# Spreading a normalisation's two parameter rows with TensorE instead of broadcasting them by DMA

## The reference

```python
def layer_norm(x, g, b):
    xf = x.astype(jnp.float32)
    mu = jnp.mean(xf, axis=-1, keepdims=True)
    var = jnp.mean(jnp.square(xf - mu), axis=-1, keepdims=True)
    y = (xf - mu) * lax.rsqrt(var + LN_EPS)
    return (y * g.astype(jnp.float32) + b.astype(jnp.float32)).astype(x.dtype)
...
    h = layer_norm(x, ln_in_g, ln_in_b)
    for l in range(DEPTH):
        h = hybrid_layer(h, ...)          # begins with x @ w_in, w_in: 1024 x IN_WIDTH
```

## Time and profile before

| | us |
|---|---|
| three runs | 2106.35, 2108.43, 2108.76 (median 2108.43) |
| the profiled execution | 2107.81 |
| its span | 2106.1 |
| PE busy in the span | 2041.2 (97%) |
| DVE, ACT, POOL busy | 1495.8, 1187.7, 715.4 |
| mean granted clock of TensorE | 0.997 of full |

### The profile page before, as it was taken

The page is one execution under the profiler, slowest core; times in us unless marked ns, Lnnn a source line. Parts: engine busy times, 40 slices in busy tenths (PEclk is TensorE's granted clock), DMA queues, the critical chain, the costliest instruction groups (busy, mean ns, idle before and its releaser), DMA issues.

```text
span 2106.1 us, 36550 instructions
## 1 busy us (share of the span) xinstructions
PE 2041.2 (97%) x11636; PEld 1744.8 (83%) x11636; DVE 1495.8 (71%) x2958; ACT 1187.7 (56%) x2023; POOL 715.4 (34%) x646
## 2 busy tenths in 40 slices
PE   8999999999999999999999999999999999999997
PEld 6987888888887888788788888888888878888886
DVE  6666768888888655655676567788888886555556
ACT  4456457766657644545444554567755685554443
POOL 1100005877874311111120000088787561111111
PEclk9999999999999999999999999999999999999999
DMA  5654546777773467667565734477777615766664
GB/s 187 205 181 132 178 151 180 188 182 189 189 183 103 134 215 226 209 223 227 178 200 169 228 114 153 166 181 189 187 183 189 186 59 182 218 221 219 226 221 144
DMA packets 179781, 384.12 MB, mean 182 GB/s; under 512 B 52528, under 2 KB 85328, under 8 KB 179696
## 3 DMA queue, kind: packets, MB, share of 16 engines
q1 hardware_dynamic: 139632, 372.26, 54.4%
q0 software_dynamic: 40064, 10.81, 6.3%
HBM read 365.04 MB, written 17.96 MB: 182 GB/s over the span
## 4 chain that ended last, share of the span: by engine, by line
PE 86%; DVE 5%; DMA 4%; ACT 2%; issue 1%; POOL 0%; SPq 0%; POOLq 0%; DVEq 0%; ACTq 0%
PE wide L1689 35%; PE acc L1675 9%; PE wide L1675 9%; PE acc L1676 5%; PE wide L1676 5%; PE acc L1663 3%; PE acc L1664 3%; PE acc L1665 3%; PE acc L2171 3%; DMA raw<-in_front 2%; PE acc L1678 1%; PE wide L1678 1%; ACT hi L680 1%; DMA gt<-table 1%; PE tr L1867 1%
## 5 line engine op out<-in xcount | busy, mean ns | idle before, releaser
L680 ACT ACTIVATE hi<-raw 128x1024 fp32r<-128x1024 f32 (+1 forms) x644 | 676.1, 1050 | 641.8 <-DMA raw<-in_peer_v 335.1
L1029 DVE TENSOR_TENSOR lo<-raw,hi 128x1024 fp32r<-128x1024 f32 x520 | 635.4, 1222 | 388.0 <-ACT hi L680 386.6
L623 POOL DMA_INDIRECT table<-picks,spots x256 | 478.7, 1870 | 263.5 <-DVE spots L1499 138.6
L1675 PE MATMUL acc<-xT,hi 128*128 128x512 f32 x896 | 321.8, 398 | 0.0
L1689 PE MATMUL wide<-hi,w_lo 128*128 128x512 f32 x1016 | 314.1, 390 | 7.3 <-DVE w_lo L1603 7.0
L1675 PE MATMUL wide<-xT,hi 128*128 128x512 f32 x868 | 311.8, 398 | 4.3 <-DVE lo L1029 4.2
L1689 PE MATMUL wide<-lo,w_hi 128*128 128x512 f32 x1016 | 313.1, 389 | 0.0
L656 POOL TENSOR_TENSOR big<-big,gt 128x128 f32 x248 | 119.5, 482 | 569.8 <-DMA gt<-table 558.0
L1689 PE MATMUL wide<-hi,w_hi 128*128 128x512 f32 x1016 | 313.1, 389 | 0.0
L1676 PE MATMUL acc<-xT,lo 128*128 128x256 f32 x1024 | 266.5, 281 | 0.0
L1676 PE MATMUL wide<-xT,lo 128*128 128x256 f32 x992 | 258.2, 281 | 0.0
(11 more groups left out here) (330 smaller groups left out, 3032.9 us busy)
## 6 DMA issues: line engine op xcount, KB each, us to landing
raw<-in_peer_u SPq DMA_DIRECT2D x256, 512.0 KB, 3.5
raw<-in_peer_v SPq DMA_DIRECT2D x254, 512.0 KB, 4.4
raw<-in_front SPq DMA_DIRECT2D x114, 512.0 KB, 3.7
table<-blank SPq DMA_DIRECT2D x16, 1024.0 KB, 7.5
gt<-table SPq DMA_DIRECT2D x254, 64.0 KB, 4.1
ln_par<-in_ln POOLq DMA_DIRECT2D x10, 512.0 KB, 5.9
raw<-in_front SPq DMA_DIRECT2D x12, 384.0 KB, 3.1
w<-in_cmp_w POOLq DMA_DIRECT2D x16, 256.0 KB, 4.2
```

The lines of the kernel that those rows point to most:

```text
L623: pool.indirect_dma_start(table[l], bass.IndirectOffsetOnAxis(spots[:, u, k:k + 1], 0), picks[:, 2, 0, u * TOPK + k:u * TOPK + k + 1], Non ...
L680: nc.scalar.activation(hi[:, s, :width], raw[:, s, :width], ACT.Identity).then_inc(hi_done, 1)
L1029: nc.vector.tensor_tensor(lo[:, s], raw[:, s], hi[:, s].bitcast(F32), ALU.subtract).then_inc(lo_done, 1)
L1675: mm(bank, hi[:, s, c], xT[:, :, k], start=k == 0, stop=False)
```

## The change

The two DMAs now bring one row each to partition 0 of `ln_par` (2 x 4 KB instead of 2 x 512 KB written). POOL first writes a row of 128 ones into `first_i[0:1, 0]` and raises `pool_step`. PE, before its twenty matmuls, waits for the row of ones and for both DMAs, and multiplies the ones (as the stationary operand, 1 x 128) by the rows (as the moving operand, 1 x 512), four matmuls in plain float32: the factors go to both banks of `acc`, the shifts to both banks of `wide[:, 1]`. It then raises `ln_spread`. DVE reads factors and shifts for this first norm from PSUM. Since `acc[:, 1]` is now taken, the twenty matmuls write into `wide[:, 0]`, and ahead of the twelve later ones (into `acc[:, 1]`) PE waits in layer 0 until DVE has read the factors for the second time. The later norms load `ln_par` as before.

```diff
@@ gpsimd
-            pst = Steps(pool, pool_step, 0, 12)
-
-            def ln_load(i):
-                for r in range(2):
-                    pool.dma_start(ln_par[:, r], t["ln"][i, r].partition_broadcast(P)).then_inc(ln_loaded, 16)
-
-            ln_load(0)
+            pst = Steps(pool, pool_step, 0, 13)
+
+            for r in range(2):
+                pool.dma_start(ln_par[0:1, r], t["ln"][0, r].unsqueeze(0)).then_inc(ln_loaded, 16)
+            pst.link(nc.gpsimd.memset(first_i[0:1, 0], 1.0))
             pst.link(nc.gpsimd.memset(ident[:], 0.0))
@@ vector: normalise(tt, nth, loads, chain, meanwhile=None)
-                dve.wait_ge(ln_loaded, loads)
+                if loads is None:
+                    dve.wait_ge(ln_spread, 1)
+                    factor, shift = acc[:].rearrange("p b n -> p (b n)"), wide[:, 1]
+                else:
+                    dve.wait_ge(ln_loaded, loads)
+                    factor, shift = ln_par[:, 0], ln_par[:, 1]
                 chain.link(nc.vector.scalar_tensor_tensor(out=xs[:, tt], in0=xs[:, tt], scalar=mv[:, tt, 0:1],
-                                                          in1=ln_par[:, 0], op0=ALU.subtract, op1=ALU.mult))
+                                                          in1=factor, op0=ALU.subtract, op1=ALU.mult))
...
-                                                   in1=ln_par[:, 1, half], op0=ALU.mult, op1=ALU.add).then_inc(x_ready, 1)
+                                                   in1=shift[:, half], op0=ALU.mult, op1=ALU.add).then_inc(x_ready, 1)
@@ tensor
+            pe_.wait_ge(pool_step, 1)
+            pe_.wait_ge(ln_loaded, 32)
+            for r, dst in enumerate((acc[:].rearrange("p b n -> p (b n)"), wide[:, 1])):
+                for h in range(2):
+                    half = slice(512 * h, 512 * h + 512)
+                    ins = mm(dst[:, half], first_i[0:1, 0], ln_par[0:1, r, half], start=True, stop=True)
+            ins.then_inc(ln_spread, 1)
             pe_.wait_ge(consts_ready, 1)
             pe_.wait_ge(masks_ready, 2)
...
-            keep_clock(acc[:, 1], 20)
+            keep_clock(wide[:, 0, :512], 20)
...
                 acc_free(l, A_LAT + 1)
+                if l == 0:
+                    pe_.wait_ge(ln_step, TT * 4)
                 keep_clock(acc[:, 1], 12)
```

More of the change, by code:

```diff
@@ L442, in build @@
         stored = sem("stored")
+        ln_spread = sem("ln_spread")
         low_copied = sem("low_copied")
@@ L1094, in _ @@
                 statistics(tt, chain)
-                normalise(tt, tt, 32, chain, first_low_parts if tt == 1 else None)
+                normalise(tt, tt, None, chain, first_low_parts if tt == 1 else None)
             chain.end()
```

## The result

Nine runs of each kernel: 2114.1 us median (2112.0 to 2118.1) for the changed kernel, 2108.1 (2105.8 to 2111.1) for the one before. The ratio is 1.0033 (95% interval 1.0024 to 1.0042): 6.0 us slower by the medians, 7.0 by the ratio, where I had forecast 2110.4 with a range up to 2113.2. The sign of the shift in my sum was right, its size was not (+6.0 against +2.3), and rival 3 (2113.8, chance 0.10) is what came, together with a later landing of the rows.

A forecast was written before the change was run, and what follows sets the result against it. PE, busy 2041.2 of 2106.1 us, was taken to bound the kernel, its twenty unread matmuls the start. Adding +2.3 us on PE's chain to 2107.8 and 2108.43 (2110.1, 2110.7) gave 2110.4 us, range 2107.4 to 2113.2.

The forecast's parts named there:

- my sum: Over the whole kernel: +2.3 us on PE's chain from the start, the other parts of the change adding nothing.
- rival 3: At the start: four one-row matmuls don't raise PE's clock, the twenty start cold; +5.6 us, time 2113.8; chance 0.10.
- The bound of the start: First tile: PE's twenty unread matmuls run until 14.49; VectorE's 2.88 us wait has 1.7 to 2.4 us of slack.
- Four float32 matmuls: Ahead of PE's twenty: 1.72 us each at 1.2 GHz, some 0.95 at 2.4 GHz; the four cost 6.3 us.
- the clock should rise 5.6 us later, at 11.5: At PE's start: clock rises 5.6 us after its first matmul at 5.9, so the twenty take 4.6 us.
- the forecast of the transposes (16.8): First tile: PE gets to its transposes at 16.8 instead of 14.49, +2.3 us.
- The landing at 5.9: At the start: the two rows on POOL's queue land at 5.9 us, with 3.9 and 6.2 as ends.
- my upper end of 6.2: At the start: latest time in us taken for the landing of the two rows.
- Hidden work: Early in the kernel: new wait, memset (about 0.3 us), PSUM inputs and less early traffic add nothing to PE's chain.
- Carried to the end: From the start to the kernel's end: +2.3 us stays, since every later link hangs on PE.

The follow-up runs named there:

- the last kernel: Changed kernel with rows loaded first by SyncE, cast by VectorE, float32r spreading, 14 unread matmuls, none before layer 0's second transposes: 2106.5 us, ratio 0.9997 against kernel before.

## Why the prediction was wrong, point by point

- *The bound of the start is PE's unread matmuls, not VectorE's wait.* Right: VectorE's wait grew from 2.9 to 7.2 us and was still covered, and with the traffic taken away and PE left alone the time stayed (1.0003). The slack was small, though: with 14 unread matmuls the chain runs through `ln_par`'s transfers.
- *Four float32 matmuls, each four times a float32r one, as two records.* Right: 0.85 us a record, 1.71 a matmul, 7.1 with the first gap. The float32r form of the same work took a quarter.
- *"If they begin at 5.9, PE's first work lies 1.3 us earlier than before (7.20), and the clock should rise 5.6 us later, at 11.5."* **This is the step that failed.** I let any matmul count towards the rise and held the twenty at 4.6 us. In every trace with work of one row ahead of the twenty the rise came behind that work: here the four ran slowly to the end (7.1 instead of 6.3 us), and the twenty began at the low clock (6.8 instead of 4.6). That is 3.0 of the 4.2 us between the forecast of the transposes (16.8) and their start (21.05). With 128 rows in the same place both took 9.7 us together, where I had said 10.9 and the changed kernel took 13.9. It is rival 3 by its own mechanism. I gave it 0.10 though I wrote that the trace held no row for or against it: without a row, nothing spoke for the other side either.
- *The landing at 5.9.* Off by 1.2 us (PE starts at 7.13), the rest of the 4.2. The bytes came when I said, from 5 us on, but the last of the queue's 64 packets started only after 6.2; I took the end of the wait too near to the first bytes, and my upper end of 6.2 was too low. Why these few bytes took so long is not shown.
- *Hidden work*: the new wait ahead of the twelve, the memset, PSUM as an input, the earlier traffic. Right, none shows.
- *Carried to the end.* Right for this loss: 6.6 at the transposes, 6.4 at the 48 matmuls, 6.0 between the medians (5.1 to 8.9 by the interval). It isn't a rule for gains: 5.2 us gained at the 48 matmuls in the last kernel were 1.1 at the end (at most 2.5 by the interval). My reason, that every later link hangs on PE, leaves out that a weight tile can then be the later one.

## What to carry to other kernels

Before moving work onto TensorE at a moment when its clock is low, ask what it costs at the low clock in its own format, and whether a trace shows that the clock rises behind work of its kind; here, work on 1 or 32 rows was slow itself and left what followed slow as well. A wait that shows in a trace is worth nothing while another engine is still busy with what comes next: find the time at which the result is taken, not the time at which it is ready. An unknown for which the trace has no row deserves a chance that shows it, and a range that holds both its ends.

## What the runs showed of the hardware that I had not expected

- Matmuls of 1 row (float32 and float32r) and of 32 rows (float32r), 7.1 us of them without a pause, ran at the low clock to their end, and the rise came only 3.3 to 6.2 us into the 128-row matmuls behind them (six traces); with 128 rows in their place (two traces, float32) the clock was up after 5.2 and 3.3 us, before the work was over.
- The granted clock reads 1.00 in the profile's windows ahead of the first rise (7.20 to 12.80 us in the earlier trace rows), while 512 columns take 0.43 us there. Only the pace tells.
- A transfer of 4 KB that POOL issued at 1.3 to 2.1 us, behind 1 MB from SyncE, took 4.9 us; issued first by SyncE, from 1.06 us on, it was there at 2.9, when VectorE began to cast it in the last kernel.
- The kernel's own spread is large against such a change: 33 runs of the kernel before on one chip lay between 2102.6 and 2112.3 us.
